# Block attention with its turns one and a half projections behind the scores, two heads' end steps moved, and weight remainders subtracted on the vector engine

## The chip, the cores and the metric

The kernel runs on one core of one Trainium2 chip. The metric is device time in microseconds (us) of one launch. The kernel before takes 2485.27 us (median of 3 runs, 2482.62 to 2485.55).

## What is computed

The reference is one inference step of a streaming encoder: two layers over 560 tokens (512 frames, 16 meta tokens, 32 tokens of a sample stream), model width 1024, in float32. Each layer is

```
h    = rmsnorm(x)
proj = h @ w_in                          # all columns of the three branches and their gates
oa   = chunk-causal attention, 8 heads, keys from a low-rank latent (branch A)
ob   = sliding-window attention, 8 heads, windows of 128, sinks, ALiBi (branch B)
oc   = gated linear attention, 4 heads, state carried along (branch C, "gla")
y    = sig(gate_a) * (oa @ w_up_a) + sig(gate_b) * (ob @ w_up_b) + sig(gate_c) * (oc @ w_up_c)
x    = x + rmsnorm(y @ w_out)
x    = x + rmsnorm(relu(rmsnorm(x) @ w_ff1)^2 @ w_ff2)
```

## The kernel before, in words

**Projections.** All weights are cut into 302 units of 128x1024 float32, 151 per layer. The SP queue loads a unit into a slot (`wraw`). ScalarE rounds it into `whi` (`w_hi`, L1194), GpSimd subtracts that from the raw unit and leaves the remainder `wlo` in the raw unit's place (`w_lo`, L2105). The activations are split into a rounded tile and a remainder in the same way (`h_hi` and `h_lo`, `oa_hi` and `oa_lo`, and so on; the helper's line is L1198 on ScalarE, L2110 on GpSimd, L1725 on VectorE for `h_lo`). TensorE (L814) forms each product as high times high, high times remainder and remainder times high. A unit is used in two halves of 280 tokens, each of 24 matmuls of 280 columns into one PSUM bank. Two banks, `dense`, always serve the projections; some of the banks that the attention uses (`att`) join them in stretches where they are free: up to `FOUR` between `qn` and `up_c`, `THREE` around block attention, `SIX` for the output projection and the MLP. A bank that is full is emptied ("evac") by VectorE or ScalarE, by the kind of unit. A gate unit's half goes through ScalarE three times, VectorE once (L1615) and ScalarE again.

**The plan.** `layer_plan` writes one list of steps, and each of the five engines walks the same list and issues what is its part of each step. ("half", u, 0) is a half of unit u, ("dense", u) both halves. The steps ("w", u), which split unit u, are put in by a rule behind a half or a dense: a unit gets its step once the last user of its slot lies at least 2 halves back. An engine works strictly in the order of this list, so a wait in one step holds up whatever its engine has in the later ones.

**Stages.** In layer 0 the profile has: start 0 to 50 us, gated linear attention with its projections to 305, preparation of branch A to 377, attention A to 558, projections of branch B to 581, block attention B with up_a, up_b and gate units to 703, the rest of the merge to 780, the output projection with the norm behind it to 865, the MLP to 1223, and the norm behind that, overlapped with the next layer's first units, to about 1270. Layer 1 has the same stages some 1227 us later. Where a norm is overlapped with the next stage's first units the text calls the place a lap.

**Block attention.** It runs over five blocks. For block i: the scores on TensorE (L1109); for each of the two tiles t (4 heads each) VectorE adds the ALiBi term while it reads the scores (L2017, four times), writes the sinks (L2022), takes the maxima (L2023, L2024); ScalarE takes the exponentials with their sums (L1501, four times); VectorE takes the reciprocals (L2031); GpSimd multiplies (L2190); TensorE transposes the probabilities ("turn t", L1120 and L1121, for the last block L1125 to L1127); VectorE copies them out of PSUM (L2038, L2039); TensorE multiplies by the values (L1144); VectorE copies `ob_raw` out (L2047), and ScalarE and GpSimd split it. Before the change the plan has for each block: scores, one dense, sums (tile 1), values of the block before, turn 0, half of a unit, turn 1, the other half.

**Gated linear attention.** For each of 4 heads there are vector steps ("v arg", "v lev", "v end", L1767, L1768, L1774, L1777) and matmul steps that stand between the projections. The first head's stand behind its own cq, ck, cv units (evictions L1626) and the last head's ("v out", "v oc", L1852, L1853) reach into the preparation of branch A, whose rotation (L1867) TensorE awaits at L984. The sums of squares of the norms are added on VectorE (L1586, L1683, L1686), and TensorE needs them at L826.

## Time and profile before

| | |
|---|---|
| median of 3 runs | 2485.27 us |
| lowest, highest | 2482.62, 2485.55 us |
| profiled execution: its time, its span | 2482.8, 2481.1 us |
| mean granted TensorE clock | 0.978 |
| TensorE busy | 2349.4 us (95%) |
| VectorE busy | 912.3 us (37%) |
| ScalarE busy | 999.6 us (40%) |
| GpSimd busy | 1067.5 us (43%) |
| chain that ended last | TensorE 82%, VectorE 9%, ScalarE 4%, GpSimd 3% |

The span is the profiled execution from its first to its last instruction. The chain that ended last is followed back from the last instruction, at each step to what released it. A busy TensorE need not be one at its peak: it has two clocks, and the granted clock tells the share of the full one.

### The profile page before, as it was taken

The numbers are of one execution on the slowest core, as the hardware profiler recorded it, in microseconds if no ns is written. First come the engines' busy times: TensorE is split into PE (matmuls) and PEld (weight loads), VectorE is DVE, ScalarE is ACT, GpSimd is POOL, SyncE is SP. The second block draws the span as 40 slices with busy tenths as digits, with TensorE's granted clock in tenths as the row PEclk, the third lists the DMA queues.
The fourth block names the chain that finished last, engine by engine and source line by source line (L and its number), as shares of the span: only waits on it lengthen the run. The fifth ranks groups of instructions, "written<-read, shape, count | busy, mean of one in ns | idle before, by whom it ended". The sixth has DMA issues, their size and how long they took to land.

```text
span 2481.1 us, 41727 instructions
## 1 busy us (share of the span) xinstructions
PE 2349.4 (95%) x17728; PEld 2215.4 (89%) x17728; DVE 912.3 (37%) x1804; ACT 999.6 (40%) x1895; POOL 1067.5 (43%) x655
## 2 busy tenths in 40 slices
PE   6999989998899899999979999899988998999997
PEld 5999968888789899999979999688977998999997
DVE  3555554543422601000463664445344135010014
ACT  4354433333345542422334443344334456424322
POOL 4444313343456364544443442144443664545442
PEclk9999999999899999999989999999999999999999
DMA  4121221112124122222321222211211241222222
GB/s 166 52 64 58 87 73 52 52 60 68 43 60 165 51 78 86 86 86 69 118 74 50 63 63 89 62 53 52 75 52 43 69 157 60 77 86 85 86 69 88
DMA packets 59368, 187.72 MB, mean 76 GB/s; under 512 B 8048, under 2 KB 17104, under 8 KB 58672
## 3 DMA queue, kind: packets, MB, share of 16 engines
q1 hardware_dynamic: 49040, 164.33, 20.8%
q10 hardware_dynamic: 10144, 20.73, 2.7%
q8 instruction: 141, 2.31, 0.4%
q14 instruction: 43, 0.35, 0.0%
HBM read 170.87 MB, written 10.89 MB: 73 GB/s over the span
## 4 chain that ended last, share of the span: by engine, by line
PE 82%; DVE 9%; ACT 4%; POOL 3%; issue 1%; DMA 0%; ACTq 0%; DVEq 0%; SPq 0%; POOLq 0%
PE dense L814 39%; PE att L814 27%; PE att L858 2%; PE att L1071 2%; PE att L997 1%; PE att L934 1%; POOL wlo L2105 1%; PE att L1017 1%; PE att L1109 1%; DVE prob L2017 1%; POOL prob L2190 1%; PE att L938 1%; PE att L920 1%; PE att L1042 1%; DVE h_lo L1725 1%
## 5 line engine op out<-in xcount | busy, mean ns | idle before, releaser
L2105 POOL TENSOR_TENSOR wlo<-wraw,whi 128x1024 fp32r<-128x1024 f32 x302 | 729.8, 2422 | 982.9 <-ACT whi L1194 982.8
L814 PE MATMUL dense<-h_hi,whi 128*128 128x280 f32 (+1 forms) x2000 | 598.7, 299 | 24.2 <-DVE h_lo L1725 9.6
L814 PE MATMUL dense<-h_lo,whi 128*128 128x280 f32 (+1 forms) x2000 | 588.6, 294 | 0.0
L814 PE MATMUL dense<-h_hi,wlo 128*128 128x280 f32 (+1 forms) x2000 | 587.6, 294 | 0.0
L1194 ACT ACTIVATE whi<-wraw 128x1024 fp32r<-128x1024 f32 x302 | 315.5, 1049 | 307.7 <-DMA wraw<-in_w 266.3
L814 PEld LDWEIGHTS dense<-h_hi,whi 128*128 128x128 f32 (+1 forms) x2000 | 381.2, 191 | 39.5 <-issue 11.8
L814 PEld LDWEIGHTS dense<-h_hi,wlo 128*128 128x128 f32 (+1 forms) x2000 | 381.0, 191 | 0.9
L814 PEld LDWEIGHTS dense<-h_lo,whi 128*128 128x128 f32 (+1 forms) x2000 | 381.3, 191 | 0.0
L814 PE MATMUL att<-h_hi,whi 128*128 128x280 f32 (+1 forms) x1040 | 310.4, 298 | 11.9 <-DVE h_lo L1725 4.4
L814 PE MATMUL att<-h_lo,whi 128*128 128x280 f32 (+1 forms) x1040 | 307.6, 296 | 0.0
L814 PE MATMUL att<-h_hi,wlo 128*128 128x280 f32 (+1 forms) x1040 | 307.3, 295 | 0.0
L814 PEld LDWEIGHTS att<-h_hi,whi 128*128 128x128 f32 (+1 forms) x1040 | 200.3, 193 | 16.0 <-ACT rstd L1402 4.9
L814 PEld LDWEIGHTS att<-h_hi,wlo 128*128 128x128 f32 (+1 forms) x1040 | 200.0, 192 | 0.4 <-issue 0.2
L814 PEld LDWEIGHTS att<-h_lo,whi 128*128 128x128 f32 (+1 forms) x1040 | 200.0, 192 | 0.0
L814 PE MATMUL att<-hid_hi,whi 128*128 128x280 f32 x672 | 195.7, 291 | 0.0
L814 PE MATMUL att<-hid_lo,whi 128*128 128x280 f32 x672 | 195.7, 291 | 0.0
L814 PE MATMUL att<-hid_hi,wlo 128*128 128x280 f32 x672 | 195.4, 291 | 0.0
L2110 POOL TENSOR_TENSOR hid_lo<-hid_raw,hid_hi 128x560 fp32r<-128x560 f32 (+1 forms) x76 | 92.0, 1211 | 191.5 <-ACT hid_hi L1198 191.5
L814 PEld LDWEIGHTS att<-hid_hi,whi 128*128 128x128 f32 x672 | 126.3, 188 | 0.1
L814 PEld LDWEIGHTS att<-hid_lo,whi 128*128 128x128 f32 x672 | 126.3, 188 | 0.0
L814 PEld LDWEIGHTS att<-hid_hi,wlo 128*128 128x128 f32 x672 | 126.2, 188 | 0.1
L1665 DVE TENSOR_TENSOR facc<-facc,att 128x280 f32<-128x280 f32 x60 | 26.7, 446 | 225.8 <-PE att L814 225.6
(341 smaller groups left out, 4478.0 us busy)
## 6 DMA issues: line engine op xcount, KB each, us to landing
wraw<-in_w SPq DMA_DIRECT2D x302, 512.0 KB, 3.6
x_spill<-x ACTq DMA_DIRECT2D x2, 2240.0 KB, 7.4
x<-x_spill ACTq DMA_DIRECT2D x2, 2240.0 KB, 12.3
k_cat<-k_rope ACTq DMA_DIRECT2D x16, 212.0 KB, 3.4
x<-in_x SPq DMA_DIRECT2D x4, 560.0 KB, 6.1
out_y_out<-x SPq DMA_DIRECT2D x4, 560.0 KB, 3.1
out_c_out<-ckv ACTq DMA_DIRECT2D x2, 560.0 KB, 7.0
state<-in_state ACTq DMA_DIRECT2D x8, 128.0 KB, 2.1
```

Source lines behind the costliest of these rows:

```text
L814: mm = pe.matmul(bank(u, o, hf)[0:m, :], a[:, k, o * 128:o * 128 + m], b[:, k, H[hf]], start=(k == 0 and i == 0), stop=(k == kt - 1 and i ...
L858: mm = pe.matmul(ps[0:rows, PAIR_BANK[i], c0:c0 + 64].rearrange("p (g t) -> p g t", t=m), e[:, 128 * sb:128 * sb + rows], late, start=(n_ ...
L920: mm = pe.matmul(ps[:, bank, 256 * (sb % 2):256 * (sb % 2) + 256], ktok[0:n, sb, :], vtok[0:n, sb, :], start=(sb % 2 == 0), stop=True, ski ...
L934: pe.matmul(dst, vtok[0:n, sb, 128 * vt:128 * vt + 128], amat[0:n, a:a + n], start=first, stop=(sb == 0), skip_group_check=True)
L938: mm = pe.matmul(dst, state[:, STATE_IN[sb], 128 * vt:128 * vt + 128], qe[:, a:a + n], start=False, stop=True, skip_group_check=True)
L997: mm = pe.matmul(ps[0:n, pair + i, 0:512], src[:, k, a:a + n], wuv[:, k, :], start=(k == 0), stop=(k == KL - 1))
L1017: mm = pe.matmul(ps[:, S0 + a, 0:META + 128 * (i + 1)], q_cat[:, h, 128 * i:128 * i + 128], k_cat[:, h, K_META:K_FRAME + 128 * (i + 1)], s ...
L1071: mm = pe.matmul(dst[64 * a:64 * a + 64, :], v[:, hc], pt(a), start=(n_ == 0), stop=(n_ == len(parts) - 1), skip_group_check=True)
L1194: act.activation(whi[slot][:, :], wraw[slot][:, :], ACT.Copy).then_inc(act_done, st.done("act", f"w hi {u}"))
L1665: ins = dve.tensor_tensor(facc[:, m, c], facc[:, m, c], src, ALU.add)
L2105: pool.tensor_tensor(wlo[slot][:, :], wraw[slot][:, :], whi[slot][:, :].bitcast(F32), ALU.subtract).then_inc(pool_done, st.done("pool", f" ...
L2110: pool.tensor_tensor(lo, raw, hi.bitcast(F32), ALU.subtract).then_inc(pool_done, st.done("pool", name))
```

## The change

**In block attention** both turns of a block now stand behind three halves of projections after its scores. The plan for block i is: scores, values of block i - 1, sums (now both tiles: the reciprocals and the normalisations of GpSimd), low (the remainder of `ob` of block i - 1, a step of its own), half u 0, half u 1, a place for splits, half v 0, turn 0, turn 1, evac v 0, a place for splits, half v 1. Half v 0 is a "guest": it goes to bank 5, which the values otherwise write, its eviction comes behind the turns, and the values of block i wait for that eviction. The first evictions of `up` units are interleaved with the score tiles. In the new step "splits" a weight unit may be split once its slot's last user lies 1 half back, instead of 2.

**At the ends of gated linear attention** head 0's vector steps are spread over the units ck 0, cv 0 and ckv (before: all behind ck 0), and the last head's "v out" and "v oc" come two and one groups of preparation steps later.

**The remainders of the weights** (`w_lo`, 302 instructions of 128x1024) go from GpSimd to VectorE. TensorE waits for VectorE's counter instead of GpSimd's.

Lines of the changed kernel are 14 further down in TensorE's part and 20 in VectorE's (L2017 is L2037), 16 in GpSimd's; `w_lo` is L1595 there.

```diff
@@ -423,6 +423,8 @@
 
             plan = []
             U_MIX, V_MLP = [UIDX["out", n] for n in range(KD - LAP, KD)], [UIDX["ff1", n] for n in range(LAP)]
+            U_B = range(UIDX["up_a", 0], UIDX["up_a", 0] + 10)
+            U_B_FIRST = [u for u in U_B[::2] if UNITS[u][0] == "up_a"]
             U_MLP, V_NEXT = [UIDX["ff2", 32 - LAP + n] for n in range(LAP)], list(range(LAP))
             JOBS = {"a": [("a", t, i) for t in range(4) for i in range(4)]}
             jobs = JOBS["a"]
@@ -462,8 +464,12 @@
                     order.append(("half", u, 1))
                     if UNITS[u][0] == "cq":
                         gla_steps((0, "v arg 1"))
-                    if UNITS[u][0] == "ck":
-                        gla_steps((0, "v lev 0"), (0, "v arg 2"), (0, "v lev 1"), (0, "v end"), (0, "v lev 2"))
+                    if UNITS[u] == ("ck", 0):
+                        gla_steps((0, "v lev 0"), (0, "v arg 2"))
+                    if UNITS[u] == ("cv", 0):
+                        gla_steps((0, "v lev 1"), (0, "v end"))
+                    if u == V_NEXT[-1]:
+                        gla_steps((0, "v lev 2"))
                 dense()
                 order.append(("prep_a", "square"))
                 dense()
@@ -517,9 +523,9 @@
                 for steps in ((1, 2), (3, 4, 5), (10, 11, 6), (7, 8, 9, 12, 13), ()):
                     dense()
                     order.extend([("prep_a", s) for s in steps])
-                    if 1 in steps:
+                    if 3 in steps:
                         gla_steps((last, "v out"))
-                    if 10 in steps:
+                    if 7 in steps:
                         gla_steps((last, "v oc"))
                 for j in range(len(JOBS["a"]) + 2):
                     order.append(("att", "a", j))
@@ -531,14 +537,15 @@
                 dense()
                 for i in range(5):
                     order.append(("b", i, "scores"))
-                    dense()
+                    if i > 0:
+                        order.append(("b", i - 1, "values"))
                     order.append(("b", i, "sums"))
                     if i > 0:
-                        order.append(("b", i - 1, "values"))
-                    order.append(("b", i, "turn 0"))
-                    u = next(dn)
-                    order.extend([("half", u, 0), ("b", i, "turn 1"), ("half", u, 1)])
-                order.append(("b", 4, "values"))
+                        order.append(("b", i - 1, "low"))
+                    u, v = next(dn), next(dn)
+                    order.extend([("half", u, 0), ("half", u, 1), ("splits",), ("half", v, 0, i), ("b", i, "turn 0"), ("b", i, "turn 1"),
+                                  ("evac", v, 0), ("splits",), ("half", v, 1)])
+                order.extend([("b", 4, "values"), ("b", 4, "low")])
                 plan.extend([(l, step) for step in order])
                 for u in range(next(dn), NU):
                     kind, n = UNITS[u]
...
@@ -618,19 +627,19 @@
                     crossing = True
                 if step[0] == "tokens" and step[2] == 1:
                     crossing = False
-                if step[0] not in ("half", "dense"):
+                if step[0] not in ("half", "dense", "splits"):
                     continue
-                now += 1 if step[0] == "half" else 2
+                now += {"half": 1, "dense": 2, "splits": 0}[step[0]]
                 if step == ("half", LAP - 1, 0) and l_ == 0:
                     begun = True
-                most = 1 if step[0] == "half" else 2
+                most = {"half": 0 if step[1:] and step[1] in U_B else 1, "dense": 2, "splits": 1}[step[0]]
                 while begun and split and most:
                     key = split[0]
                     was = slot_before[key]
                     g_ = guard_of.get(key)
                     if crossing and begun_at[key] - now > 5:
                         break
-                    if (was is not None and done_at[was] + 2 > now) or (g_ is not None and done_at[g_] + 2 > now):
+                    if (was is not None and done_at[was] + (1 if step[0] == "splits" else 2) > now) or (g_ is not None and done_at[g_] + 2 > now):
                         break
                     full.append((key[0], ("w", key[1])))
                     assert now + 2 <= begun_at[key], (key, now, begun_at[key])
...
                 kind = UNITS[u][0]
                 wide = kind in ("out", "ff1", "ff2") or u in V_NEXT
-                b = min(SIX if wide else FOUR if UIDX["qn", 1] <= u <= UIDX["up_c", 0] else THREE if UIDX["qb", 1] <= u < UIDX["out", 0] else TWO, key=lambda c: bank_free[c])
+                b = 5 if key in guests else min(SIX if wide else FOUR if UIDX["qn", 2] <= u <= UIDX["up_c", 0] else THREE if UIDX["qb", 1] <= u < UIDX["out", 0] else TWO, key=lambda c: bank_free[c])
                 bank_of[key] = DENSE_BANKS[b]
                 before[key] = bank_user[b]
...
+                    lent[l_, "values", guests[key]] = key
+                if b in FOUR[2:] and UIDX["qn", 2] <= u <= UIDX["up_c", 0]:
...
@@ -760,6 +771,9 @@
 
                 def wait_bank(u, o, hf):
                     prev = before[l, u, o, hf]
+                    if (l, u, o, hf) in guests:
+                        i = guests[l, u, o, hf]
+                        pe.wait_ge(dve_done, A("dve", f"b o {i - 1}" if i > 0 else f"a o {len(jobs) - 1}"))
                     if prev is not None:
                         pl, pu, po, ph = prev
                         e = evac_engine(UNITS[pu][0])
...
                     hi_x, lo_x = moving[src]
                     halved = src in ("h", "h2")
                     pe.wait_ge(act_done, A("act", f"w hi {u}"))
-                    pe.wait_ge(pool_done, A("pool", f"w lo {u}"))
+                    pe.wait_ge(dve_done, A("dve", f"w lo {u}"))
                     if kind == "qn" and n == 1:
                         pe.wait_ge(act_done, A("act", f"gla rstd {C_HEADS - 1}"))
...
 
                 def b_values(i):
                     pe.wait_ge(dve_done, A("dve", f"b turned {i} 1"))
-                    if i > 0:
-                        pe.wait_ge(dve_done, A("dve", f"b o {i - 1}"))
+                    _, pu, po, ph = lent[l, "values", i]
+                    pe.wait_ge(dve_done, A("dve", f"evac {pu} {po} {ph}"))
                     if i < 4:
                         r = slice(0, key_count("b", i) - 128)
...
                     ins.then_inc(dve_done, st.done("dve", name))
                     dve.wait_ge(dve_done, st.count["dve"])
 
+                def w_lo(u):
+                    slot = slot_of[l, u]
+                    dve.wait_ge(act_done, A("act", f"w hi {u}"))
...
-                            if t == 0 and up is not None:
-                                evac(up, [0], (0, 1))
-                    if what in ("scores", "sums"):
-                        t = 0 if what == "scores" else 1
-                        sm = stat[0:rows, t, :]
-                        dve.wait_ge(act_done, A("act", f"b exp {i} {t}"))
-                        dve.reciprocal(sm[:, 12:16], sm[:, 8:12]).then_inc(dve_done, st.done("dve", f"b rsum {i} {t}"))
+                            if up is not None:
+                                evac(up, [t], (0,))
+                    if what == "sums":
+                        for t in range(2):
+                            sm = stat[0:rows, t, :]
+                            dve.wait_ge(act_done, A("act", f"b exp {i} {t}"))
+                            dve.reciprocal(sm[:, 12:16], sm[:, 8:12]).then_inc(dve_done, st.done("dve", f"b rsum {i} {t}"))
                     if what.startswith("turn"):
                         t = int(what[-1])
                         dve.wait_ge(pe_done, A("pe", f"b turn {i} {t}"))
...
                         evac(step[1], [1] if early else None, (0, 1))
                     elif step[0] == "half":
+                        if len(step) == 3:
+                            evac(step[1], [] if step[1] in U_B_FIRST and step[2] == 0 else None, (step[2],))
+                    elif step[0] == "evac":
                         evac(step[1], None, (step[2],))
+                    elif step[0] == "w":
+                        w_lo(step[1])
                     elif step[0] == "square":
...
                         lo_tile(oa_lo[:, t, :], oa_raw[:, t, :], oa_hi[:, t, :], f"oa lo {t}", f"oa hi {t}")
                 def b(i, what):
-                    if what in ("scores", "sums"):
-                        t = 0 if what == "scores" else 1
-                        pool.wait_ge(dve_done, A("dve", f"b rsum {i} {t}"))
-                        pb = prob_b(i, t)
-                        rows, w = pb.shape[0], pb.shape[2]
-                        rs = stat[0:rows, t, 12:16].rearrange("p (a n) -> p a n", n=1).to_broadcast([rows, B_G, w])
-                        pool.tensor_tensor(pb, pb, rs, ALU.mult).then_inc(pool_done, st.done("pool", f"b prob {i} {t}"))
-                    if what == "values":
+                    if what == "sums":
+                        for t in range(2):
+                            pool.wait_ge(dve_done, A("dve", f"b rsum {i} {t}"))
+                            pb = prob_b(i, t)
+                            rows, w = pb.shape[0], pb.shape[2]
+                            rs = stat[0:rows, t, 12:16].rearrange("p (a n) -> p a n", n=1).to_broadcast([rows, B_G, w])
+                            pool.tensor_tensor(pb, pb, rs, ALU.mult).then_inc(pool_done, st.done("pool", f"b prob {i} {t}"))
```

**Order of GpSimd, block attention, from the last tile of block 0 to block 1.** `prob_142` is tile 0, `prob_143` tile 1. Before:

```order
L2190 TENSOR_TENSOR prob_143<-prob_143,stat 128x580
L2105 TENSOR_TENSOR wlo_63<-wraw_50,whi_76 128x1024
L2190 TENSOR_TENSOR prob_142<-prob_142,stat 128x836
L2105 TENSOR_TENSOR wlo_64<-wraw_51,whi_77 128x1024
L2190 TENSOR_TENSOR prob_143<-prob_143,stat 128x836
L2110 TENSOR_TENSOR ob_lo<-ob_raw,ob_hi 128x4x128
L2124 TENSOR_TENSOR y<-y,sig 128x560 x2
L2105 TENSOR_TENSOR wlo_62<-wraw_49,whi_75 128x1024
```

Now:

```order
L2206 TENSOR_TENSOR prob_143<-prob_143,stat 128x580
L2140 TENSOR_TENSOR y<-y,sig 128x560 x2
L2206 TENSOR_TENSOR prob_142<-prob_142,stat 128x836
L2206 TENSOR_TENSOR prob_143<-prob_143,stat 128x836
L2126 TENSOR_TENSOR ob_lo<-ob_raw,ob_hi 128x4x128
L2140 TENSOR_TENSOR y<-y,sig 128x560 x2
```

The weight remainders that stood between the normalisations are gone, and the two normalisations of a block follow each other.

**Order of VectorE, the same block.** `ob_raw` is the output of the block before, `ptf` the transposed probabilities. Before:

```order
L2023 TENSOR_REDUCE stat<-prob_143 128x4
L2024 TENSOR_SCALAR stat<-stat 128x4
L2031 RECIPROCAL stat<-stat 128x4
L1615 SCALAR_TENSOR_TENSOR sig<-att,sig 128x280
L1615 SCALAR_TENSOR_TENSOR sig<-dense,sig 128x280
L2031 RECIPROCAL stat<-stat 128x4
L2047 COPY ob_raw<-att 128x4x128
L2038 COPY ptf<-att 128x512
L2039 COPY ptf<-att 80x512
```

Now:

```order
L2044 TENSOR_SCALAR stat<-stat 128x4
L2067 COPY ob_raw<-att 128x4x128
L2051 RECIPROCAL stat<-stat 128x4 x2
L1635 SCALAR_TENSOR_TENSOR sig<-dense,sig 128x280 x2
L1595 TENSOR_TENSOR wlo_63<-wraw_50,whi_76 128x1024
L2058 COPY ptf<-att 128x512
L2059 COPY ptf<-att 80x512
L2058 COPY ptf_second<-att 128x512
L1635 SCALAR_TENSOR_TENSOR sig<-att,sig 128x280
L1595 TENSOR_TENSOR wlo_64<-wraw_51,whi_77 128x1024
L1635 SCALAR_TENSOR_TENSOR sig<-att,sig 128x280
```

Both reciprocals now follow the output copy, and a weight remainder stands between the gates and the transposed copies.

**Order of VectorE, start of layer 1, first head.** `level` tiles are the head's decay factors, `cproj_116` the evicted projections. Before:

```order
L1621 TENSOR_SCALAR cproj_116<-att 128x280
L1767 TENSOR_TENSOR level<-level,cproj_116 128x4x64
...
L1767 TENSOR_TENSOR level<-level,cproj_116 128x140x2
L1768 TENSOR_TENSOR level<-level,cproj_116 128x140x2
L1774 TENSOR_TENSOR level<-level,cproj_116 128x280
L1626 COPY cproj_116<-att 128x280
L1626 COPY cproj_116<-dense 128x280
L1637 COPY ckv<-dense 128x280 x3
```

Now:

```order
L1641 TENSOR_SCALAR cproj_116<-att 128x280
L1595 TENSOR_TENSOR wlo_72<-wraw_59,whi_85 128x1024
L1787 TENSOR_TENSOR level<-level,cproj_116 128x4x64
L1788 TENSOR_TENSOR level<-level,cproj_116 128x4x64
...
L1646 COPY cproj_116<-dense 128x280
L1787 TENSOR_TENSOR level<-level,cproj_116 128x16x16
...
L1646 COPY cproj_116<-dense 128x280
L1657 COPY ckv<-att 128x280
L1787 TENSOR_TENSOR level<-level,cproj_116 128x70x4
L1788 TENSOR_TENSOR level<-level,cproj_116 128x70x4
```

The evictions of the projections (L1626, now L1646) stood behind all pairs of levels, and now stand between them.

## Rows read from the trace of the kernel before

**Rows 1.** The page: busy time, share of the span and instructions of each engine.

```profile
PE 2349.4 (95%) x17728; PEld 2215.4 (89%) x17728; DVE 912.3 (37%) x1804; ACT 999.6 (40%) x1895; POOL 1067.5 (43%) x655
```

**Rows 2.** Waits of TensorE over the whole span: engine, line, releaser: us, times, longest.

```profile
PE att L1120 <- POOL prob L2190: 33.7, 14, 5.5
PE att L826 <- DVE nsum L1686: 20.0, 6, 10.9
PE att L984 <- DVE rtmp L1867: 12.3, 2, 6.2
PE att L1125 <- POOL prob L2190: 11.0, 2, 5.5
PE dense L814 <- DVE cproj L1626: 7.6, 1, 7.6
```

**Rows 3.** Groups by form: name, shapes, count | busy us, mean ns | idle before, releaser.

```profile
L2105 POOL TENSOR_TENSOR wlo<-wraw,whi 128x1024 fp32r<-128x1024 f32 x302 | 729.8, 2422 | 982.9 <-ACT whi L1194 982.8
L1194 ACT ACTIVATE whi<-wraw 128x1024 fp32r<-128x1024 f32 x302 | 315.5, 1049 | 307.7 <-DMA wraw<-in_w 266.3
L1586 DVE TENSOR_TENSOR nsum<-nsum 128x280 f32<-128x280 f32 x56 | 46.5, 830 | 38.9 <-ACT nsum L1275 38.2
L1725 DVE TENSOR_TENSOR h_lo<-h_raw,h_hi 128x560 fp32r<-128x560 f32 x24 | 16.9, 730 | 0.0
```

**Rows 4.** Stretches: start:end, us, busy and instructions of PE, PEld, DVE, ACT, POOL, clock, DMA.

```profile
50.00:305.00 255.00, 252.09 (x1951) 239.45 (x1951) 135.77 (x260) 110.01 (x163) 107.24 (x97) 0.99 0.21 64
581.00:703.00 122.00, 98.65 (x750) 88.49 (x751) 55.77 (x136) 50.03 (x142) 49.53 (x30) 0.91 0.15 44
865.00:1223.00 358.00, 358.00 (x2790) 358.00 (x2790) 35.97 (x66) 128.20 (x193) 186.78 (x94) 1.00 0.28 87
```

**Rows 5.** The same view around one late turn of block 2.

```profile
639.57:642.89 3.32, 3.32 (x27) 3.09 (x25) 1.51 (x5) 2.25 (x6) 0.00 (x0) 1.00 0.10 39
642.89:647.65 4.76, 0.00 (x0) 0.00 (x0) 1.63 (x3) 2.87 (x6) 3.94 (x3) 0.92 0.00 0
647.65:654.51 6.86, 6.86 (x33) 6.62 (x33) 1.28 (x2) 0.00 (x0) 1.18 (x1) 0.56 0.01 2
```

**Rows 6.** VectorE, timeline of block 2: start, us, operation, [idle before <-releaser].

```profile
630.64 1.22 DVE L2017 SCALAR_TENSOR_TENSOR prob<-const,att 128x208 f32<-128x208 f32 x4 [1.96 <-PE att L1109]
636.13 0.17 DVE L2031 RECIPROCAL stat<-stat 128x4 f32<-128x4 f32 x1
642.14 0.17 DVE L2031 RECIPROCAL stat<-stat 128x4 f32<-128x4 f32 x1
```

**Rows 7.** ScalarE and GpSimd, timeline of the same block.

```profile
638.00 0.19 ACT L1501 ACTIVATION_READ_ACCUMULATOR prob<-prob,stat 128x1 f32 x1
643.71 2.35 POOL L2105 TENSOR_TENSOR wlo<-wraw,whi 128x1024 fp32r<-128x1024 f32 x1 [5.75 <-ACT whi L1194]
646.02 1.58 POOL L2190 TENSOR_TENSOR prob<-prob,stat 128x836 f32<-128x836 f32 x1
```

**Rows 8.** Start of layer 1, timeline: VectorE, GpSimd, TensorE.

```profile
1286.60 0.42 DVE L1767 TENSOR_TENSOR level<-level,cproj 128x256 f32<-128x256 f32 x1
1286.94 2.61 DVE L1768 TENSOR_TENSOR level<-level,cproj 128x256 f32<-128x256 f32 x1
1286.86 2.41 POOL L2105 TENSOR_TENSOR wlo<-wraw,whi 128x1024 fp32r<-128x1024 f32 x1 [2.47 <-ACT whi L1194]
1296.64 0.57 PE L814 MATMUL dense<-h_hi,whi 128*128 128x280 f32 x1 [7.60 <-DVE cproj L1626]
```

**Rows 9.** Lap behind the mixers, timeline: ScalarE, VectorE.

```profile
847.77 1.04 ACT L1194 ACTIVATE whi<-wraw 128x1024 fp32r<-128x1024 f32 x1
847.99 3.62 DVE L1703 SCALAR_TENSOR_TENSOR mix<-mix,par,rstd 128x280 f32<-128x280 f32 x2
```

**Rows 10.** Lap behind the MLP, timeline: VectorE, ScalarE.

```profile
1246.55 1.03 DVE L1586 TENSOR_TENSOR nsum<-nsum 128x280 f32<-128x280 f32 x2
1247.01 1.04 ACT L1194 ACTIVATE whi<-wraw 128x1024 fp32r<-128x1024 f32 x1
```

More of the change, by code:

```diff
@@ L565, in program @@
                 layer_plan(l_)
-            halves = []
+            halves, guests = [], {}
             for l_, step in plan:
                 if step[0] == "half":
+                    if len(step) > 3:
+                        guests[l_, step[1], outs_of(UNITS[step[1]][0])[0] - 1, step[2]] = step[3]
                     halves.extend([(l_, step[1], o, step[2]) for o in range(outs_of(UNITS[step[1]][0])[0])])
@@ L653, in program @@
                 bank_free[b], bank_user[b] = i + 1, key
-                if b in FOUR[2:] and UIDX["qn", 1] <= u <= UIDX["up_c", 0]:
+                if key in guests:
+                    lent[l_, "values", guests[key]] = key
+                if b in FOUR[2:] and UIDX["qn", 2] <= u <= UIDX["up_c", 0]:
                     lent[l_, b] = key
@@ L1576, in link @@
                     dve.wait_ge(dve_done, st.count["dve"])
+                def w_lo(u):
+                    slot = slot_of[l, u]
+                    dve.wait_ge(act_done, A("act", f"w hi {u}"))
+                    dve.tensor_tensor(wlo[slot][:, :], wraw[slot][:, :], whi[slot][:, :].bitcast(F32), ALU.subtract
+                                      ).then_inc(dve_done, st.done("dve", f"w lo {u}"))
                 def add_square(u, hf):
@@ L2050, in leads @@
                 def leads(step):
-                    return step[0] == "att" or (step[0] == "b" and step[2] == "scores")
+                    return step[0] == "att"
                 for at_step, (l, step) in enumerate(order):
@@ L2081, in _ @@
                         early = after[0] == "dense" and UNITS[after[1]][0] in ("up_a", "up_b")
-                        if step[0] == "att":
-                            att(step[1], step[2], after[1] if early else None)
-                        else:
-                            b(step[1], step[2], after[1] if early else None)
+                        att(step[1], step[2], after[1] if early else None)
                     elif step[0] == "b":
-                        b(step[1], step[2], None)
+                        b(step[1], step[2], U_B[2 * step[1]] if U_B[2 * step[1]] in U_B_FIRST else None)
                     elif step[0] == "split_y":
@@ L2100, in link @@
                     pool.wait_ge(pool_done, st.count["pool"])
-                def w_lo(u):
-                    slot = slot_of[l, u]
-                    pool.wait_ge(act_done, A("act", f"w hi {u}"))
-                    pool.tensor_tensor(wlo[slot][:, :], wraw[slot][:, :], whi[slot][:, :].bitcast(F32), ALU.subtract
-                                       ).then_inc(pool_done, st.done("pool", f"w lo {u}"))
                 def lo_tile(lo, raw, hi, name, hname):
@@ L2197, in _ @@
                         evac(step[1], (0, 1) if step[0] == "dense" else (step[2],))
-                    elif step[0] == "w":
-                        w_lo(step[1])
                     elif step[0] == "masks":
```

1 line of the change is left out of this document (added).

## The prediction

> **What bounds the kernel now.** I read the page first: TensorE is busy 95% of the span, VectorE 37%, GpSimd 43% [rows 1]. The reader is to see that only idle or slow time of TensorE can be won: no change of the other engines pays unless TensorE waits for them. So the next view is TensorE's waits over the whole span [rows 2]. The largest is for GpSimd's normalisation in block attention: 33.7 us at L1120 and 11.0 us at L1125, 44.7 us in all. Then come the sums of the norms (20.0 us at L826), the rotation before branch A (12.3 us at L984, 6.2 the longest) and one wait of 7.6 us at the start of layer 1. All gaps of TensorE above 0.3 us come to 118 us. The stretches [rows 4] say where: in block attention TensorE is busy for 98.65 of 122 us (23.4 idle) at a granted clock of 0.91, while the MLP is busy for all of its 358 us.
>
> **Block attention.** I then followed block 2 on each engine. VectorE starts on the scores at 630.64 and is done with both tiles at 636.13 [rows 6]; ScalarE's exponentials of tile 1 end at 638.19 [rows 7]. But the second reciprocal runs only at 642.14, because two gate evictions stand ahead of it in VectorE's order [rows 6], and GpSimd takes a weight remainder of 2.35 us first, at 643.71, so the normalisation runs from 646.02 to 647.60 [rows 7]. TensorE is idle from 642.89 to 647.65 [rows 5]. After it the clock is 0.56 for 6.86 us [rows 5]: TensorE had idled 4.76 us and falls to its lower level, 1.2 instead of 2.4 GHz. 33 matmuls take 6.86 us where the 24 projection matmuls in it would take 3.3 (3.32 in the stretch ahead of the gap) and 8 transposes some 0.9: 2.7 us more. The same happens behind the other long gaps of the stage, 9.3 us per layer when I add the four slow pieces. So 22.3 us of waiting for GpSimd and 9.3 us of slow clock stand in each layer, 63 us in both.
>
> With the change the normalisations need both reciprocals (they follow the copy of the previous output) but no gates and no remainder stands ahead of them. From the end of the scores: both tiles 5.5 us (636.13 less 630.64), plus one `up` eviction of 0.45, exponentials to 7.6 us (638.19 less 630.64), reciprocal 0.17, the first normalisation beside it, the second 1.58: about 9.4 us, and 10.2 if both run one behind the other from 7.0. TensorE has the values (2.0 us) and three halves of 3.25 us ahead of the turns, 11.75 us; before it had one dense and the values, or one half, between them. So 1.5 us are left and both turns should not wait. What is late next is the transposed copy: it is needed for the values, behind the scores of the next block, and has half v 1 (3.25 us) and the scores (2.46 us) to run beside; it takes four copies of 0.7 us. I take a gain of 28 us per layer, 56 us in all: the 31.6 us less the restart gaps of 0.7 us at the first scores and about 3 us that single blocks may still lose. The bounds: at best all 63 us; at worst one remainder of 1.2 us and a late `up` eviction in each of the ten blocks cost 2 us each with slow clock, leaving 43 us.
>
> **The weight remainders.** GpSimd loses 302 times 2.42 us, 729.8 us [rows 3], and falls to about 338 us busy. No row shows this subtraction on VectorE. Upper bound: a same-kind subtraction of 560 columns takes 0.73 us [rows 3], 1024 columns by proportion 1.33. Lower bound: ScalarE's pass over the same tile, 1.05 us [rows 3]. I take 1.2, since a part of the 0.73 us is fixed. VectorE gains 362 us of work. It also loses some waiting: where GpSimd subtracts beside it, VectorE's two-input instructions stretch. At 1286.94 the `level` product took 2.61 us, its like just ahead 0.42, beside the remainder from 1286.86 to 1289.27 [rows 8]; the square sums average 830 ns [rows 3] where the plain ones take 0.44 to 0.45; at 847.99 two L1703 take 3.62 us instead of 0.92 [rows 9]. Over all such groups I count 60 to 100 us. So VectorE ends near 1190 us, 48% of the span: it does not bound the kernel by its sum.
>
> The Trainium skill ("SBUF — State Buffer", section "Who interferes with whom") states that VectorE and GpSimd share one pair of ports as an exclusive lock, which an instruction of VectorE with two SBUF inputs meets whenever GpSimd reads SBUF, and that the one that comes second waits for the whole of the first. By that rule, with which the 2.61 us agree, the new subtraction takes the same lock: it can be held up by GpSimd's `hid_lo` and normalisations, and hold them up. The sum above goes by the rows; what the rule could make of it at its worst is rival (b).
>
> **Starts of the layers.** At layer 1 the evictions of cv 0 stand behind all `level` products and end at 1296.5; TensorE is idle 7.60 us and starts slow [rows 8]. The changed order evicts after the third pair. The need is at about 1290, so I leave 1.4 us of gap, and win 6.2 us plus 2.6 us of slow clock (behind the gap 96 matmuls took 15.1 us, at full clock 12.4): 9 us. Layer 0 has the same place with a gap of 2.20 us and 1.6 us slow: 3 us. At the very start one wait of 3.1 us for a remainder on GpSimd shrinks by the difference of 1.2 us: 2 us with its follower. Sum 14 us, bounds 8 and 17.
>
> **The last head.** "v out" leaves the way of the rotation, so the 6.2 us at L984 [rows 2] should shrink to about 3.5 us; but a remainder now stands ahead of the key eviction a little later, and waits for a rounding there: about 2.6 us given back. I count this 0, from 4 us gain to 3 us loss per layer.
>
> **The laps.** Here VectorE's chain is on the path (20.0 us at L826) [rows 2]. A remainder in it costs 1.2 us or the wait for ScalarE's rounding: 847.77 to 848.81 against a VectorE free at 847.99 [rows 9]; and at the MLP's lap a remainder comes between the two square sums that begin at 1246.55, while the rounding ends at 1248.05 [rows 10], so the second sum ends some 1.5 us later. The relief of the lock (3.62 to 0.92) pays part. I take a loss of 1.4 us per lap behind the mixers, two of them, and 2.1 us at the one between the layers: 5 us, bounds 0 and 12.
>
> **GLA and the MLP.** In heads 1 to 3 VectorE is busy 53% (135.77 of 255 us) [rows 4] and some 50 remainders of both layers add 12% of the stretch; TensorE has only two banks there, 3.25 us of cover per half. I cost them at nothing since the evictions of 0.44 us behind a 1.2 us remainder fit in 3.25 us; without this cover each costs up to 1.2 us. In the MLP VectorE is busy for 35.97 of 358 us [rows 4]: nothing.
>
> **Sum.** 2482.8 (the profiled execution's own time; its span is 2481.1, the median of the runs is 2.5 higher) less 56, less 14, plus 5 gives 2417.8. Against the median that is 2420. I add 2 us for what small waits a fuller VectorE may bring in GLA: **2422 us**.
>
> **Rivals.** (a) VectorE becomes the late one in GLA. A remainder must wait for ScalarE's `whi`, and evictions stand behind it. GpSimd waited 982.8 us in all for that rounding [rows 3], harmlessly, as nothing urgent was behind; VectorE has everything behind it. It decides where the rounding ends more than 1.6 us (3.25 less 1.2 less 0.44) after VectorE arrives. Should it happen at each of 50 units with 1.5 us and slow clock behind some, 75 us go and the kernel lands at 2422 plus 75, 2497: slower. Against it: ScalarE is busy only 110 of 255 us there [rows 4]. 4%, of which 1 is the case that it just eats the gain. (b) The lock. If the new subtraction usually meets a GpSimd instruction and takes 2.4 us as GpSimd's did, VectorE gets 360 us more, GLA loses 0.5 us per unit and the turns 1 us each: about 45 us of the gain go, 2465. For it speaks the stretch by the lock that the rows show; against it that GpSimd is then busy 14% of the time. 8%. (c) The turns no longer wait but the values do, for the transposed copies or the guest's eviction: a gain of only a third in block attention, 19 instead of 56 us: 2457. 13%. (d) The forecast, 75%, own range 2408 to 2440.
>
> **How the numbers follow.** The forecast's range plus half of (b) and (c): 2405 to 2456. A measurement of this kernel can tell some 0.2%, 5 us, from no change. (b), (c) and (d) are faster, less 2% for their far ends: 0.94; within 0.2% 0.03, these 2% and the 1% of (a); slower 0.03, the rest of (a).
>
> **What would show it.** Right: waits at L1134 and L1139 (now) for GpSimd below 8 us of 44.7; granted clock in block attention at 0.98; the group of `wlo` on VectorE with 302 times 1.1 to 1.4 us; GpSimd near 340 us busy; the 7.6 us wait below 2; the waits at L840 for the sums of squares 20 to 26 us. Wrong: a wait of TensorE for `wlo` on VectorE or for evictions of a few us per unit in GLA, or values waiting for the turned copies.

## The result, and the profile after

The changed kernel takes 2423.19 us (median of 4 runs, 2417.29 to 2426.14), against 2483.94 us before (median of 4 runs, 2478.45 to 2485.55). The ratio is 0.9756, with a 95% interval from 0.9731 to 0.9782. The prediction was 2422 us.

The page of the profiled execution (span, engines, granted clock), whose own time is 2417.29 us:

```profile
span 2415.6 us, 41753 instructions
PE 2325.6 (96%) x17728; PEld 2194.9 (91%) x17728; DVE 1176.0 (49%) x2106; ACT 998.8 (41%) x1895; POOL 361.5 (15%) x353
PEclk9999999999999999999989999999999999999999
```

Against [rows 1], GpSimd falls from 1067.5 to 361.5 us busy and VectorE rises from 912.3 to 1176.0 us. TensorE's 23.8 us less of busy time are matmuls that run at the higher clock; the mean granted clock goes from 0.978 to 0.99. Its gaps above 0.3 us come to 77.3 us where they were 118.1.

TensorE's waits over the whole span that the text uses (engine, line, releaser: us, times, longest), which answer to [rows 2]:

```profile
PE att L840 <- DVE nsum L1706: 20.3, 6, 11.0
PE dense L828 <- ACT h_hi L1212: 8.5, 7, 2.9
PE att L998 <- DVE rtmp L1887: 7.0, 2, 3.5
PE att L1005 <- DVE k_cat L1930: 5.7, 2, 3.0
PE att L1158 <- DVE sig L1675: 4.3, 2, 2.1
PE att L1123 <- DVE ptf_second L2059: 4.3, 4, 1.8
PE att L1056 <- POOL prob L2194: 2.2, 2, 1.1
PE dense L828 <- DVE cproj L1646: 2.0, 1, 2.0
```

The 44.7 us for GpSimd's normalisation in block attention are gone: no row of L1134 or L1139 is left. The 7.6 us for L1626 (now L1646) are 2.0, the 12.3 us at L984 (now L998) are 7.0. Three waits for VectorE are new: L1005, L1158 and L1123. At the norms the wait for `h_hi` is 8.5 us where it was 3.5. The sums of the norms stay, 20.3 us.

The groups that answer to [rows 3] (busy us, mean ns), and the stretch of block attention, which answers to the third line of [rows 4]:

```profile
L1595 DVE TENSOR_TENSOR wlo<-wraw,whi 128x1024 fp32r<-128x1024 f32 x302 | 395.1, 1311 | 495.8 <-ACT whi L1208 495.2
L1606 DVE TENSOR_TENSOR nsum<-nsum 128x280 f32<-128x280 f32 x56 | 24.9, 444 | 2.6 <-ACT nsum L1289 2.3
L1788 DVE TENSOR_TENSOR level<-level,cproj 128x256 f32<-128x256 f32 x24 | 10.1, 421 | 0.0
```

```profile
572.00:668.00 96.00, 90.99 (x773) 82.28 (x772) 64.25 (x147) 49.74 (x142) 29.63 (x20) 1.00 0.20 61
```

The remainder takes 1311 ns on VectorE, against 2422 on GpSimd. VectorE's square sums fall from 830 to 444 ns. Taking both: 395.1 us of remainders came in, yet VectorE's busy time rose by 263.7 only, so 131 us of its other instructions' time went. GpSimd is left with 361.5 us where 1067.5 less 729.8 would be 337.7: its other instructions got 23.8 us longer (a product for `y` 1654 ns in the mean, before 1388). Block attention takes some 96 us where it took some 122, TensorE idles 5.0 of them, and the clock is 1.00 instead of 0.91.

**Where the time went.** I compare the start of the same matmul in both traces at the borders of the stages (first levels of a head, first scores, first sum of squares). Each entry is the change of a stage's length in us against the kernel before; a column adds up to the difference of the spans, to rounding. The two right columns belong to experiments told below.

| stage | changed kernel | remainders back on GpSimd | block order alone |
|---|---|---|---|
| start and first head, layer 0 | -5.6 | -0.3 | +1.7 |
| heads 1 to 3, layer 0 / 1 | 0.0 / 0.0 | 0.0 / 0.0 | 0.0 / 0.0 |
| preparation to branch B's projections, layer 0 / 1 | -3.1 / +0.1 | -3.6 / -4.5 | 0.0 / +0.1 |
| block attention and merge, layer 0 / 1 | -27.2 / -28.5 | -34.2 / -35.6 | -34.2 / -35.6 |
| lap behind the mixers, layer 0 / 1 | +1.1 / +1.1 | 0.0 / 0.0 | 0.0 / -0.8 |
| lap behind the MLP | +2.7 | 0.0 | 0.0 |
| first head, layer 1 | -6.5 | -7.9 | -0.2 |
| MLP of layer 1, last norm | +0.3 | +0.8 | 0.0 |
| span | -65.5 | -85.3 | -69.0 |

Each column is one execution. That of the changed kernel is its fastest of four (2417.29 us, the median is 2423.19), the other two lie near their medians: in the table they differ from the changed kernel by 19.8 and 3.5 us, between medians by 24.5 and 9.2.

The preparation shows how much one execution can differ. A kernel told below, d4, has the same order of instructions as the changed kernel up to block attention, and TensorE has nearly the same two gaps there (layer 0: 3.5 and 3.0 us in the changed kernel, 3.9 and 3.0 in d4; layer 1: 3.5 and 2.7 in both). Yet the granted clock of the stretch (the column behind the engines) is 1.00 in one execution and 0.90 in the other; in layer 1 it is 0.97 and 0.90. First the changed kernel, then d4, the preparation of layer 0:

```profile
316.00:369.00 53.00, 46.48 (x237) 34.21 (x236) 27.16 (x49) 17.66 (x36) 0.00 (x0) 1.00 0.27 71
316.00:369.00 53.00, 46.03 (x203) 32.88 (x203) 26.01 (x46) 17.67 (x36) 0.00 (x0) 0.90 0.26 70
```

So the row "preparation to branch B's projections", -3.1 and +0.1 here, is +1.5 and +3.2 in d4's trace. The whole runs say the same: the changed kernel's four have granted clocks of 0.990, 0.989, 0.987 and 0.986 at 2417.3, 2421.4, 2425.0 and 2426.1 us. A difference of up to 5 us in a row with such gaps need not be the work of an edit.

### The profile page after: what moved, and what is told of

It is laid out like the page before. It is cut to its first block, busy times and chain, and to the rows that moved or that the text cites. A ratio compares the mean times of both kernels' runs of the same rounds, so it can differ in the third digit from the quotient of the medians.

```text
span 2415.6 us, 41753 instructions
## 1 busy us (share of the span) xinstructions
PE 2325.6 (96%) x17728; PEld 2194.9 (91%) x17728; DVE 1176.0 (49%) x2106; ACT 998.8 (41%) x1895; POOL 361.5 (15%) x353
## 4 chain that ended last, share of the span: by engine, by line
PE 81%; DVE 9%; ACT 6%; issue 2%; POOL 1%; DMA 0%; DVEq 0%; ACTq 0%; SPq 0%; POOLq 0%
PE dense L828 39%; PE att L828 26%; PE att L872 2%; PE att L1085 2%; ACT whi L1208 1%; PE att L1011 1%; PE att L948 1%; PE att L1031 1%; DVE h_raw L1756 1%; DVE wlo L1595 1%; PE att L952 1%; PE att L934 1%; PE att L1056 1%; DVE prob L2037 1%; DVE h_lo L1745 1%
## 5 line engine op out<-in xcount | busy, mean ns | idle before, releaser
L1595 DVE TENSOR_TENSOR wlo<-wraw,whi 128x1024 fp32r<-128x1024 f32 x302 | 395.1, 1311 | 495.8 <-ACT whi L1208 495.2
L828 PE MATMUL dense<-h_hi,whi 128*128 128x280 f32 (+1 forms) x1952 | 583.0, 299 | 21.3 <-ACT h_hi L1212 8.5
L828 PE MATMUL dense<-h_lo,whi 128*128 128x280 f32 (+1 forms) x1952 | 574.1, 294 | 0.0
L828 PE MATMUL dense<-h_hi,wlo 128*128 128x280 f32 (+1 forms) x1952 | 573.0, 294 | 0.0
L828 PEld LDWEIGHTS dense<-h_hi,whi 128*128 128x128 f32 (+1 forms) x1952 | 371.5, 190 | 40.2 <-ACT h_hi L1212 17.2
L828 PEld LDWEIGHTS dense<-h_hi,wlo 128*128 128x128 f32 (+1 forms) x1952 | 371.3, 190 | 0.6
L828 PE MATMUL att<-h_hi,whi 128*128 128x280 f32 (+1 forms) x1088 | 321.2, 295 | 5.4 <-ACT h_hi L1212 2.6
L828 PE MATMUL att<-h_lo,whi 128*128 128x280 f32 (+1 forms) x1088 | 318.5, 293 | 0.0
L828 PE MATMUL att<-h_hi,wlo 128*128 128x280 f32 (+1 forms) x1088 | 318.0, 292 | 0.0
L2194 POOL TENSOR_TENSOR prob<-prob,stat 128x288 f32<-128x288 f32 (+4 forms) x40 | 51.6, 1296 | 475.3 <-DVE stat L2021 475.3
## 6 DMA issues: line engine op xcount, KB each, us to landing
x<-x_spill ACTq DMA_DIRECT2D x2, 2240.0 KB, 12.1
```

Source lines behind the costliest of these rows:

```text
L828: mm = pe.matmul(bank(u, o, hf)[0:m, :], a[:, k, o * 128:o * 128 + m], b[:, k, H[hf]], start=(k == 0 and i == 0), stop=(k == kt - 1 and i ...
L1595: dve.tensor_tensor(wlo[slot][:, :], wraw[slot][:, :], whi[slot][:, :].bitcast(F32), ALU.subtract).then_inc(dve_done, st.done("dve", f"w l ...
L2194: pool.tensor_tensor(pb[0:rows, :, :], pb[0:rows, :, :], rs, ALU.mult).then_inc(pool_done, st.done("pool", f"{br} prob {j}" if tile == til ...
```

## The experiments

Each ran beside the kernel before on one chip; c, d and e were three such rounds on three chips. Medians are of 4 runs (c2: 10); the kernel before had medians of 2481.9 to 2482.9 us there, and 2483.9 beside the changed kernel, which was not run again. A difference between kernels of different rounds is uncertain by these 1 to 2 us too. First the three parts of the change were taken apart.

**c1: the remainders back on GpSimd.** The rest as changed.

```diff
-                    pe.wait_ge(dve_done, A("dve", f"w lo {u}"))
+                    pe.wait_ge(pool_done, A("pool", f"w lo {u}"))
...
-                    dve.tensor_tensor(wlo[slot][:, :], wraw[slot][:, :], whi[slot][:, :].bitcast(F32), ALU.subtract
+                    pool.tensor_tensor(wlo[slot][:, :], wraw[slot][:, :], whi[slot][:, :].bitcast(F32), ALU.subtract
```

> The changed kernel with only the weight remainders back on GpSimd. Theory (the place of the turns is what pays): the normalisations have 11.75 us of cover and no remainder stands between them, so block attention keeps most of its gain (waits for GpSimd's normalisation below 10 us of 44.7); the laps win back about 5 us; time 2415 to 2435. Rival (what pays is that GpSimd is rid of 730 us of remainders, which delayed it and stretched VectorE's instructions): the waits for GpSimd come back at 15 us per layer with slow clock behind them, time 2455 to 2475.

Measured: 2398.72 us, ratio 0.9654 (0.9639 to 0.9668). That is 24.5 us less than the changed kernel, and below the range of either theory. Page and largest waits of TensorE:

```profile
span 2395.8 us, 41749 instructions
PE 2324.4 (97%) x17728; PEld 2195.6 (92%) x17728; DVE 907.5 (38%) x1804; ACT 998.6 (42%) x1895; POOL 1068.5 (45%) x655
```

```profile
PE att L840 <- DVE nsum L1700: 20.1, 6, 11.0
PE dense L828 <- DVE h_lo L1739: 9.7, 9, 2.3
PE att L998 <- DVE rtmp L1881: 5.9, 2, 2.9
```

GpSimd is as busy as before (1068.5 us), the square sums and levels stretch again, and no wait for GpSimd's normalisation in block attention is among the rows: once the turns stand three halves back, 730 us of remainders on GpSimd cost nothing there. So the order of the turns pays, and the move of the remainders is a loss. My theory had the direction and undervalued both.

**c2: the remainders alone on VectorE.** The kernel before with `w_lo` moved; turns and heads as before.

> The kernel before with only the weight remainders moved to VectorE; turns and heads as before. Theory: one late turn per block is late by the remainder of 2.35 us and by the gates ahead of the reciprocal; without the remainder a gap of 4.8 us shrinks to about 1 to 2.5 us and its slow clock mostly goes; 15 us per layer are won, less 5 us in the laps: 2455 to 2465. Rival (the order of the turns alone decides): under 10 us won, 2475 to 2490. Other rival (the remainders are the whole gain): 2425 to 2435.

Measured: 2477.77 us, ratio 0.9979 (0.9969 to 0.9988), 5.1 us gained. The theory fell, the first rival held. The waits at the turns, and block 2's late turn on VectorE, GpSimd and TensorE:

```profile
PE att L1120 <- POOL prob L2192: 23.9, 14, 4.5
PE att L1125 <- POOL prob L2192: 11.5, 4, 4.5
```

```profile
639.65 1.23 DVE L1581 TENSOR_TENSOR wlo<-wraw,whi 128x1024 fp32r<-128x1024 f32 x1 [1.45 <-ACT whi L1194]
640.79 0.17 DVE L2037 RECIPROCAL stat<-stat 128x4 f32<-128x4 f32 x1
641.04 1.58 POOL L2192 TENSOR_TENSOR prob<-prob,stat 128x836 f32<-128x836 f32 x1 [7.09 <-DVE stat L2037]
642.68 0.42 PE L1120 MATMUL att<-const,prob 128*80 128x128 f32 x1 [3.21 <-POOL prob L2192]
```

35.4 of 44.7 us stay, and block attention and merge gained 6.5 and 8.2 us where the expectation had 15 per layer. The remainder has left the place ahead of GpSimd's normalisation and stands now ahead of the reciprocal on VectorE, where it waits 1.45 us for ScalarE's rounding and takes 1.23. The normalisation runs at 641.04, and TensorE idles 3.2 us in place of 4.76 [rows 5]. A remainder that moves to another engine moves into that engine's queue: I had left its new place out of this expectation.

**c3: the heads' end steps back**, and **c4: block attention back** (each in the changed kernel, by its hunks of the diff).

> The changed kernel with the first and last head's steps as before. Theory: the 7.6 us wait at the start of layer 1 comes back at 6 to 9 us with slow clock, the 2.2 us one of layer 0 too, and branch A's rotation waits 6 us again: 10 to 16 us more than the changed kernel, 2433 to 2439. Rival (relief of the lock on the level products had removed that wait anyway): within 5 us of the changed kernel.

> The changed kernel with block attention in its old order (remainders on VectorE and heads as changed). Theory: the remainders on VectorE keep part of the gain, 2440 to 2455; it lies 10 to 16 us below the kernel with the remainders alone moved. Rival (the order of the turns alone decides): 2465 to 2480.

Measured: c3 2436.71 us, ratio 0.9806 (0.9791 to 0.9820); c4 2470.13 us, ratio 0.9942 (0.9925 to 0.9959). The heads are worth 13.5 us with the new block order (as expected) and 7.6 us with the old one (c4 against c2), less than the 10 to 16 expected; no run shows why. c4 went to its rival: without the new order 12.8 us of some 60 are left.

**d1: the new block order alone.** The heads as before, the remainders on GpSimd.

> The kernel before with the new order of block attention alone; heads and remainders as before. Theory (the new order pays 70 us by itself, the heads pay 8 us more, and the remainders on VectorE cost 24 us): 2403 to 2412. Rival (heads and block order depend on each other): above 2415.

Measured: 2413.96 us, ratio 0.9722 (0.9708 to 0.9737): between the two ranges, 2 us above the theory's. One part of the change alone beats all three together. The heads are worth 15.2 us on top (c1 against d1), not 8, which the table places: 7.7 us at layer 1's first head, 2.0 at layer 0's, 3.6 and 4.6 in the preparations, less 1.6 in the last lap and the last norm (16.3 between the two profiled executions). Block attention and merge give 34.2 and 35.6 us in both kernels, so heads and block order do not depend on each other there.

**d2: remainders on VectorE at the start only.** c1, but VectorE takes those of layer 0's first units. The expectation says 11 units; the edit moves nine (VectorE has 1813 instructions where c1 has 1804).

```diff
+            def on_vector(l_, u):
+                return l_ == 0 and u < UIDX["cq", 1]
...
+                    e = "dve" if on_vector(l, u) else "pool"
+                    pe.wait_ge(by_name[e], A(e, f"w lo {u}"))
```

> The changed kernel with the remainders back on GpSimd except those of layer 0's first 11 units, which VectorE takes. Theory (only at the start is a faster remainder on the path: 5.3 us there between the two traces): 2390 to 2396, below the kernel with all remainders on GpSimd (2398.7). Rival (start gains came by chance from the clock): 2397 to 2401.

Measured: 2392.06 us, ratio 0.9633 (0.9617 to 0.9649), as the theory said. Start and first head are 5.7 us shorter than before, with c1 0.3. TensorE's gaps there come to 19.2 us, with c1 22.8. This is the fastest kernel of the study: 31.1 us below the changed kernel.

**d3: remainders on VectorE beside block attention only** (`on_vector` returns `u in U_B`, 20 remainders in both layers).

> The changed kernel with the remainders back on GpSimd except those of the 10 units that block attention runs beside. Theory (about 7 us per layer of the 24 us arise in block attention and the merge behind it, where VectorE waits for the rounding with copies and evictions behind): 2406 to 2413. Rival (the cost arises where VectorE is fuller as a whole, in the gated linear attention and the laps): 2398 to 2402.

Measured: 2402.08 us, ratio 0.9676 (0.9661 to 0.9690), 3.4 us above c1. Its number is at the rival's upper end (2402). Its place is the theory's, but with a third of the 7 us per layer: block attention and merge lose 2.2 and 2.3 us against c1, and this wait of TensorE is back as in the changed kernel:

```profile
PE att L1128 <- DVE ptf_second L2064: 4.2, 4, 1.7
```

The other 4.8 us per layer go by this comparison to the remainders of later units, which d3 leaves on GpSimd: in the changed kernel they stand ahead of the last block's copies (2.1 us at L1158) and ahead of evictions in the merge (four gaps of 0.38 us per layer).

**d4: the remainder behind the copies.** The changed kernel; VectorE takes the remainders of the first place for splits only behind both turned copies and the guest's eviction.

```diff
                     elif step[0] == "evac":
                         evac(step[1], None, (step[2],))
+                        for u in held:
+                            w_lo(u)
+                        held.clear()
                     elif step[0] == "w":
-                        w_lo(step[1])
+                        ahead = next(s_ for _, s_ in order[at_step:] if s_[0] != "w")
+                        if len(ahead) == 4:
+                            held.append(step[1])
+                        else:
+                            w_lo(step[1])
```

> The changed kernel, in which VectorE takes the remainder that stands ahead of the transposed copies only behind both copies and the guest's eviction. Theory (the place costs, not the 1.2 us of work): the waits of 2.1, 1.75 and 0.37 us at the values and the scores go and their slow clock with them, 5 to 12 us less than the changed kernel, 2411 to 2418. Rival (VectorE is short of time in sum): 2421 to 2426.

Measured: 2412.97 us, ratio 0.9715 (0.9700 to 0.9729), 10.2 us below the changed kernel, as the theory said; block attention and merge are 4.5 us shorter in each layer. TensorE's waits for VectorE:

```profile
PE att L998 <- DVE rtmp L1887: 7.4, 2, 3.9
PE att L1005 <- DVE k_cat L1930: 5.7, 2, 3.0
PE att L828 <- DVE sig L1675: 1.6, 4, 0.4
```

The rows of L1158 and L1123 for VectorE's copies are gone; the evictions of the merge still cost 1.6 us at `att` and as much at `dense`. VectorE does the same 302 remainders (1172.8 us busy), so for these 10.2 us it was the place and not the sum that cost. The 14.3 us from d4 down to c1 are not settled by it.

**e1: remainders on VectorE in the laps only** (9 of them), and **e2: from the second head to branch B's projections only** (96).

> The changed kernel with the remainders back on GpSimd except the nine whose steps lie in the laps (between the first scale of a norm and the last). Theory (between the two traces the laps lose 1.1, 2.7 and 1.1 us): 4 to 6 us more than with all remainders on GpSimd (2398.7), 2402 to 2405. Rival (the laps' loss comes from other remainders around them): 2398 to 2401.

> The changed kernel with the remainders back on GpSimd except the 96 whose steps lie from the second head of the gated linear attention to the projections of branch B, in both layers. Theory (the heads lose nothing although VectorE is fullest there; preparation and branch A lose 4 to 5 us per layer by the eviction that waits behind a rounding at L1930 and by one late normalisation): heads 0, in all 2403 to 2409. Rival a (VectorE too full in the heads): above 2415.

Measured: e1 2400.92 us, ratio 0.9673 (0.9657 to 0.9689); e2 2406.21 us, ratio 0.9702 (0.9677 to 0.9727). e1 lies in the rival's range, 2.2 us above c1, and the runs of the two kernels overlap (2398.7 to 2401.9 and 2394.6 to 2400.1). In its trace the laps lose 0.5, 2.1 and 0.5 us against c1, 3.1 of the 4.9 us of the changed kernel: the rest would then come from remainders just around the laps, which no run moved alone. e2 lies in the theory's range. Its heads take as long as before to 0.1 us in both layers, and the two waits that the changed kernel has in the preparation and in branch A stand there:

```profile
PE att L1014 <- DVE k_cat L1939: 5.3, 2, 2.7
PE att L1065 <- POOL prob L2210: 2.2, 2, 1.1
```

e2's runs lie far apart (2400.5 to 2410.9, at granted clocks of 0.993 to 0.986), so its 7.5 us above c1 are a rough number; its profiled one is the fastest, and in it the preparations lose 1.6 and 3.1 us against c1, not the 4 to 5 per layer of the theory.

The places that were tried alone come to -6.7, +3.4, +2.2 and +7.5 us against c1. With the 9.6 us of the later units in block attention and merge that makes 16 of the 24.5 us that the remainders cost; where the other 8 or so arise, the runs do not show. No run moved the remainders of the output projection and the MLP alone.

## Why the prediction was right

The time was met within 1.2 us. The mechanism of the main term, turns that no longer wait for the normalisations, came as worked out. That the sum fits so closely is in part luck: the gain of the block order and the loss by the remainders were both undervalued and offset each other, and the gain at the start of layer 0 came from another part of the change than forecast.

**Block attention**, forecast 56 us for both layers: 55.7 came. The turns did what was worked out. In block 2 the scores ended at 610.74 (started at 608.28, 2.46 us long) and the second normalisation ends at 620.85, 10.1 us later (10.2 was the late estimate). On VectorE, ScalarE, GpSimd and TensorE of the changed kernel, block 2 (the last line is the scores of block 3):

```profile
616.80 0.17 DVE L2044 TENSOR_SCALAR stat<-stat 128x4 f32<-128x4 f32 x1
618.96 0.18 DVE L2051 RECIPROCAL stat<-stat 128x4 f32<-128x4 f32 x1 [1.31 <-ACT prob L1515]
624.94 1.23 DVE L1595 TENSOR_TENSOR wlo<-wraw,whi 128x1024 fp32r<-128x1024 f32 x1 [1.45 <-ACT whi L1208]
627.88 0.68 DVE L2059 COPY ptf_second<-att 80x512 f32<-80x512 f32 x1
623.87 1.04 ACT L1208 ACTIVATE whi<-wraw 128x1024 fp32r<-128x1024 f32 x1
617.73 3.12 POOL L2206 TENSOR_TENSOR prob<-prob,stat 128x836 f32<-128x836 f32 x2 [4.50 <-DVE stat L2051]
628.61 2.46 PE L1123 MATMUL att<-kb,qb 64*128 64x16 f32 x32 [1.75 <-DVE ptf_second L2059]
```

But the term was a gain of 69.8 us, above the 63 that I had called the best, less 14.1 us by the remainders (c1 and d1 against the changed kernel). From 63 down to 56 I had left 7 us for all losses. That the difference was 55.7 is luck. As to the 69.8: by the stage's length 34.2 and 35.6 us went per layer, of which 22.6 is idle time (23.35 less the 0.75 us that c1 keeps), so slow running came to 11.6 to 13 us where I had counted 9.3 (four slow pieces; it is the size that was off). And the step "what is late next" had an error: I gave the transposed copies half v 1 and the next scores as cover. The rows show that the scores themselves wait for the copies (they write the same banks), so the cover is one half. The remainder at 624.94 waits 1.45 us for the rounding that ends at 624.91, takes 1.23, the copies end at 628.56, and the scores start 1.75 us late at 628.61. The 3 us that "single blocks may still lose" were meant for this, from the wrong cover. The prediction named "values waiting for the turned copies" as a sign of being wrong, and at L1158 and L1123 it came in small, 8.6 us over both layers.

**Starts of the layers**, 14 us: 5.6 and 6.5, 12.1 us. In layer 0 the forecast had 3 us for the heads' order and 2 for the faster remainder. It was the remainder alone: c2 and c3, which have the old order of the heads, gain 5.6 and 5.7 us there (d2: 5.4 us against c1), and the gap of 2.2 us is 0.3 in both. In layer 1 it is the heads' order (d1 has nothing of it): 7.9 us in c1, of which the changed kernel keeps 6.5.

**The last head**, 0: -3.1 and +0.1 in this execution, +1.5 and +3.2 in d4's, by the clock behind the same gaps. The steps behind it were right: the rotation's wait went from 6.2 to 3.5 us, and 3.0 us came back at L1005 behind a key eviction. Without the remainders (c1) the heads' move gives 3.6 and 4.5.

**The laps**, a loss of 1.4, 1.4 and 2.1 us: 1.1, 1.1 and 2.7.

**Gated linear attention and MLP**, 0: 0.0 in all heads, e2 alone too, and 0.0 in the MLP of layer 0. (In e2's trace the MLP stages are 1.5 us longer each, though it moved no remainder there.) Rival (a) did not come there. The prediction's reason, the cover of 3.25 us by two banks, fits; no run varied it. It came in small where the cover was thinner, at the turned copies, the key eviction and the laps, always in the same form: VectorE waits for a rounding with urgent work behind.

**Rival (b), the lock.** The remainder took 1311 ns on average with a median of 1226, a least of 1206 and a longest of 2294 (the view of the tile); 68 of 302 took over 1.3 us. The forecast's 1.2 us held for most, 2.4 did not. The relief on the other side was larger than the 60 to 100 us I counted, 131 us. It bought little: the wait at the start of layer 1, 7.6 us before, is 5.5 in c2 with the same order of the heads. c1 has none of the relief and is 24.5 us faster. The Trainium skill ("SBUF — State Buffer", section "Who interferes with whom") says that a VectorE instruction with two SBUF inputs contends with a GpSimd instruction that reads SBUF. The traces agree: the same square sums take 830 ns beside GpSimd's remainders and 444 without them. What such a stretch costs is what waits for the stretched instruction, in this kernel mostly nobody.

**Why layer 1 gains 1.4 us more** in block attention than layer 0 with the new order (35.6 and 34.2): the new kernels take the same time in both layers (206.1 us in the changed one, 199.0 in c1), but the kernel before takes 233.2 and 234.6. It has a gap of 2.0 us at the same turn in both, and only in layer 1 did the clock fall behind it. Layer 0, then layer 1, the 6.1 us behind that gap:

```profile
596.90:603.00 6.10, 6.09 (x62) 5.88 (x64) 1.73 (x3) 1.72 (x4) 0.00 (x0) 1.00 0.15 34
1824.40:1830.50 6.10, 6.10 (x40) 5.72 (x41) 1.28 (x2) 0.76 (x2) 0.00 (x0) 0.72 0.00 0
```

The 0.28 of the clock that is missing there is 1.7 us, an estimate from this row.

What stays open: what decides whether the clock falls behind a gap of 2 to 4 us; no run was made for it.

## What to carry to other kernels

A long instruction that is moved to a faster engine takes its wait along: ask not whether the new engine has time in sum, but what is queued behind the instruction at each place and when its input is ready. A change of several parts should be taken apart even when its result is as forecast; here one part of three ate 24.5 us of what the others gave, and of the places that were tried only the first nine of the 302 remainders gained by the faster engine.

## What the runs showed of the hardware

Where TensorE has no long gaps, the same stage of different kernels agrees within 0.1 us (34.2 and 35.6 us gained in five kernels, 0.0 in heads 1 to 3 of all of them), so that 1 us can be placed there by comparing the starts of the same matmuls, while whole runs of one kernel lie 1.6 to 10 us apart. Where it has gaps of 2 to 4 us this fails: c1 and d2 have the same instructions in the preparation of layer 1 and differ by 1.6 us (-4.5 and -6.1), the changed kernel and d4 by 4.7 us in layer 0, and the rows above show the clock that does it. And a wait of TensorE shows only part of its cost: the changed kernel's gaps shrank by 40.8 us, the span by 65.5, the rest being matmuls that no longer run at the lower clock behind a gap (the granted clock in block attention was 0.91, then 1.00).
